# Moving 24 accumulating DRAM transfers of a fused two-block kernel out of its mixers on GpSimd's queue

## The reference, cut to what matters

```python
x = x + rms_norm(mix, ln_post_mix)          # norm 1, "post"
h = rms_norm(x, ln_pre_ffn)                 # norm 1, "pre"
f = (silu(h @ w_gate) * (h @ w_up)) @ w_down
x = x + rms_norm(f, ln_post_ffn)
```

## Time and profile before

| | us |
|---|---|
| median of 3 runs | 1268.55 |
| lowest and highest | 1266.91 and 1269.29 |
| the profiled execution, whole | 1270.42 |
| its span, first to last instruction | 1268.7 |
| PE busy in the span | 1254.4 |
| POOL busy in the span | 512.3 |

### The profile page before, as it was taken

One profiled execution on the slowest core, in us unless ns is written; L12 is line 12 of the kernel. 1 busy time (PEld: TensorE's weight loads), 2 busy tenths in 40 slices (PEclk: granted clock), 3 DMA queues, 4 the chain that ended last, 5 costly groups with the idle time before them and its releaser, 6 DMA issues.

```text
span 1268.7 us, 22131 instructions
## 1 busy us (share of the span) xinstructions
PE 1254.4 (99%) x7684; PEld 1142.8 (90%) x7684; DVE 949.8 (75%) x1732; ACT 729.0 (57%) x1437; POOL 512.3 (40%) x578
## 2 busy tenths in 40 slices
PE   8999999999999999999999999999999999999998
PEld 7999978989999988889999999889889999887887
DVE  6687765799988878884566778457987777789754
ACT  5666744545555556656667778435455555556452
POOL 5576781256655500126788866310121313000000
PEclk9999999999999999999999999999999999999999
DMA  7699732335444467522377953232323333565221
GB/s 232 223 202 235 170 92 100 99 132 202 165 132 165 142 239 217 141 76 76 67 159 139 166 105 89 95 103 90 100 83 93 103 98 99 197 242 166 68 99 67
DMA packets 145607, 173.45 MB, mean 137 GB/s; under 512 B 25420, under 2 KB 111643, under 8 KB 145522
## 3 DMA queue, kind: packets, MB, share of 16 engines
q1 hardware_dynamic: 129600, 145.15, 35.8%
q0 software_dynamic: 15920, 27.18, 12.1%
q10 hardware_dynamic: 2, 0.00, 0.0%
HBM read 170.22 MB, written 39.85 MB: 166 GB/s over the span
## 4 chain that ended last, share of the span: by engine, by line
PE 88%; DVE 6%; POOL 2%; ACT 1%; DMA 1%; issue 1%; ACTq 0%; DVEq 0%; POOLq 0%
PE ps L2844 13%; PE ps L2845 13%; PE ps L2846 13%; PE ps L2963 6%; PE ps L2970 6%; PE ps L2965 6%; PE ps L3096 3%; PE ps L3100 3%; PE ps L3098 3%; PE ps L3140 3%; PE ps L3142 3%; PE ps L3141 3%; PE ps L3058 2%; DVE w_lo L2393 2%; PE ps L3046 1%; PE ps L3047 1%
## 5 line engine op out<-in xcount | busy, mean ns | idle before, releaser
L2844 PE MATMUL ps<-h_hi,w_hi 128*128 128x256 f32 (+1 forms) x748 | 238.3, 319 | 0.0
L2845 PE MATMUL ps<-h_lo,w_hi 128*128 128x256 f32 (+1 forms) x748 | 237.4, 317 | 0.0
L2846 PE MATMUL ps<-h_hi,w_lo 128*128 128x256 f32 (+1 forms) x748 | 237.2, 317 | 0.0
L2963 PE MATMUL ps<-w_hi,h_hi 128*128 128x384 f32 (+2 forms) x512 | 162.6, 328 | 0.0
L2965 PE MATMUL ps<-w_hi,h_lo 128*128 128x384 f32 (+2 forms) x512 | 157.9, 319 | 0.0
L2846 PEld LDWEIGHTS ps<-h_hi,w_lo 128*128 128x128 f32 x748 | 142.6, 191 | 9.6
L2844 PEld LDWEIGHTS ps<-h_hi,w_hi 128*128 128x128 f32 x748 | 142.6, 191 | 9.1 <-DVE h_lo L2140 0.3
L2845 PEld LDWEIGHTS ps<-h_lo,w_hi 128*128 128x128 f32 x748 | 142.7, 191 | 8.5
L1281 POOL TENSOR_TENSOR w_lo<-w_raw,w_hi 128x384 fp32r<-128x384 f32 (+2 forms) x114 | 120.5, 1131 | 26.9 <-ACT w_hi L1524 26.7
L2970 PE MATMUL ps<-w_lo,h_hi 128*128 128x384 f32 (+2 forms) x512 | 101.5, 319 | 0.0
L3140 PE MATMUL ps<-w_hi,st_hi 128*128 128x512 f32 x252 | 98.6, 391 | 0.5 <-DVE st_lo L2404 0.2
(11 more groups left out here) (327 smaller groups left out, 3338.9 us busy)
## 6 DMA issues: line engine op xcount, KB each, us to landing
w_raw<-in_w_up_dram SPq DMA_DIRECT2D x25, 1024.0 KB, 5.3
w_raw<-in_w_in_dram SPq DMA_DIRECT2D x69, 256.0 KB, 4.1
w_raw<-in_w_gate_dram SPq DMA_DIRECT2D x11, 1024.0 KB, 5.3
down_sums<-in_w_down_dram SPq DMA_DIRECT2D x18, 512.0 KB, 5.9
down_sums<-in_w_down_dram SPq DMA_DIRECT2D x36, 256.0 KB, 6.0
down_sums<-in_w_down_dram POOLq DMA_DIRECT2D x12, 768.0 KB, 8.3
down_sums<-down_sums POOLq DMA_DIRECT2D x12, 768.0 KB, 8.7
w_raw<-in_w_out_dram SPq DMA_DIRECT2D x8, 1024.0 KB, 5.1
```

Source lines behind the costliest of these rows:

```text
L2844: pe.matmul(out_, s_hi, m_hi, start=first and n == 0, stop=False, skip_group_check=True)
L2845: pe.matmul(out_, s_hi, m_lo, start=False, stop=False, skip_group_check=True)
L2846: mm = pe.matmul(out_, s_lo, m_hi, start=False, stop=last and n == len(pairs) - 1, skip_group_check=True)
L2963: pe.matmul(bank, h_hi[:, kb0 + i, tok], hi[:, i, :], start=half == 0 and i == 0, stop=False, skip_group_check=True)
```

## The change

The transfers are no longer issued inside the mixers. Those of the first product go behind mixer 0: T1 and T3 of all groups ahead of the gain loads, T2 between the gain loads and norm 1, T4 behind norm 1. Those of the second go behind norm 3: T1 and T3 ahead of the first weight sums of the mixed gate and value products, T2 behind these, T4 behind the second. The loop over the other sums starts at 2 in place of 1.

```diff
-ADD_ORDER = ((0, "T1"), (0, "T3"), (0, "T2"), (1, "T1"), (0, "T4"), (1, "T3"),
-             (1, "T2"), (2, "T1"), (1, "T4"), (2, "T3"), (2, "T2"), (2, "T4"))
-ADD_AFTER = ((9, 12, 15, 18, 20, 23, 25, 27, 29, 32, 35, 38), (8, 11, 14, 17, 20, 23, 26, 29, 32, 35, 38, 41))
...
-                        normed_units += 1
-                        if normed_units in ADD_AFTER[mx.b]:
-                            sums_added(mx.b, *ADD_ORDER[ADD_AFTER[mx.b].index(normed_units)])
...
+            def sums_of_groups(d, *names):
+
+                for name in names:
+                    for g in range(GROUPS):
+                        sums_added(d, g, name)
...
             mixer(mixers[0])
+            sums_of_groups(0, "T1", "T3")
             pool.wait_ge(shared_filled, n1.n["shared"])
             gain(1, gain_post[:, :], "ln_post_mix")
             gain(2, gain_pre[:, :], "ln_pre_ffn")
+            sums_of_groups(0, "T2")
             norm(1, True)
+            sums_of_groups(0, "T4")
             block_sums(0, 0, first=True)
...
             norm(3, False)
+            sums_of_groups(1, "T1", "T3")
             gate_sums(0, first=True)
-            with pool.Fori(1, N_MIXED) as q:
+            sums_of_groups(1, "T2")
+            gate_sums(1)
+            sums_of_groups(1, "T4")
+            with pool.Fori(2, N_MIXED) as q:
                 gate_sums(q)
```

More of the change, by code:

```diff
@@ L1285, in mixer @@
                 own_n, own_d = mx.cnt.of[mx.steps[0]]["N"], 0
-                normed_units = 0
                 for s in mx.orders["pool"]:
```

## The result

The changed kernel takes 1289.49 us in the median of 4 runs (1287.62 to 1289.72); beside it the kernel before took 1268.92. The ratio is 1.0166 (95% interval 1.0152 to 1.0180): 20.6 us slower, where 15.2 were forecast.

A forecast was written before the change was run, and what follows sets the result against it. The prediction took PE to bound the kernel, busy 1254.4 of 1268.7 us. Its terms, -4.9 (mixers) + 20.1 (norm 1) + 0 (other places) = +15.2 us, took the median from 1268.55 to 1283.8 us, range 1270 to 1290.

The forecast's parts named there:

- The chain of the forecast: Norm 1: six transfers queued ahead make `gain_post` late, then DVE, then PE's first turn; the whole delay arrives, +20.1 us.
- the 3.4 us of cover: Norm 1: first `h_tok` ready at 215.3, PE's first turn at 218.76; the forecast said this 3.4 us isn't kept.
- signs of being wrong: `gain_post` landing within 10 us, PE's turn stall far shorter than DVE's wait, or new stalls in the second block's mixed products.
- The delay: Norm 1: `gain_post` lands at 229.3, DVE wants it at 209.22; 20.1 us late, between 11.3 and 24.3.
- The pitch of 4.5 us: POOL's DMA queue before norm 1: each 768 KB accumulating transfer takes 4.5 us, bounds 4.1 and 5.2; six take 27.0.
- the term of SP's loads: Ahead of `gain_post`: SP's loads of w_gate and w_up take 6.4 us of the same engines, all within the transfers' time.
- The order that rows showed: POOL's DMA queue: a load behind an accumulating transfer waits for it; a table load landed in 7.3 us against 3.1.
- the estimate in the prediction: Norm 1 by the skill's fit: six transfers in 10.8 us, `gain_post` at 213.1, delay 4 us, sum -0.9.
- The mixers: PE's `prob` stalls go, 2.9 and 0.3 us, and a half-clock stretch, 1.7 us: -4.9 us in all.
- The other new places: T2 before norm 1, T4 behind it, and the second block's transfers: PE waits for no load, 0 us, between 0 and 6.
- Rival 3: Data of T2 and T4 delay loads for either block's first sums, up to 6 us more: +25.4, 1294 us; chance 6%.

## Why the prediction was right, and where its sizes were off

**The mechanism.** The chain of the forecast stands: transfers ahead on POOL's queue, `gain_post` late, DVE's norm 1 late, the turn late, PE idle, and the whole delay kept. Of its signs, it said that DVE would wait about 20 us (19.69), `gain_post` take some 30 us (30.2), PE have one stall of about 17 us (13.9, which is the smaller delay of 17.4 less the 3.4 us of cover), and the second turn hide the slow stretch; all are in the trace. One of its signs of being wrong is there too: new stalls in the mixed products. Two experiments show the queue's part: another queue brings 30.2 to 8.0 us, and half the number ahead brings it to 15.5.

**The delay: 20.1 us forecast, 17.4 measured.** The pitch of 4.5 us was right: the three T1 landed 4.5 us apart in the mean. Too large was the term of SP's loads, added in full with 6.4 us. The three T3, which ran beside these loads, took 16.5 us, where three at the pitch of the T1 take 13.5, so the loads cost about 3 there. One reason is that by 222 us SP's queue had moved only 1.61 of the 2.10 MB; that the two queues also overlap is likely (over 189 to 222 us they had 89.8% and 17.2% of the engines, together more than 100%), but not shown, since a transfer alone can show a share above 100% as well. Against that, the first T1 took 0.5 us longer than its term.

The order that rows showed was right. The Trainium skill's fit for a transfer of this queue, 2.0 us and bytes at 436 GB/s (DMA: Bandwidth & Descriptors, "Anatomy of one DMA"), would by the estimate in the prediction have given a delay of 4 us. The trace doesn't agree for transfers that add within DRAM, 4.5 us each against the fit's 1.8 us of data, and the measurement decides. For plain copies within DRAM, 2.9 us each here, the fit is too short as well.

**The mixers: -4.9 us forecast, -4.3 and -1.3 in the traces, but only about 2 in the medians.** The mechanism was right for the first stall: moving one T4 takes it away. The size was read from one execution with a long stall and a slow stretch. Mixer 1 gave 1.3 us where I counted only PE's wait of 0.3, and moving its last T4 alone doesn't take that wait away.

**The other new places: 0 us forecast, +5.6 measured.** This is the step that failed: "PE waits for no load there, ACT's and DVE's splits and full buffers lie between. I put it at 0, between 0 and 6 us". A load that PE doesn't wait for had no 4 to 7 us to spare: the second 512 KB load went from 4.3 to 11.4 us and the 1 MB load from 6.6 to 13.5, and all of the cover was used up. Of the two kernels that move only transfers of the second product, one shows that the stalls don't come from the first block, the other that the T4s alone make the later one. Rival 3, with a chance of 6%, named this cost; it was wrong only in the delay of 24.3 us that it was added to. The same kind of loss stands behind norm 1, 6.4 us, but was covered by the gain's delay in the changed kernel; it showed when the gains no longer waited.

**What the trace doesn't hold.** In the traces the kernel is 17.2 us slower, in the medians 20.6. Some 2 us of the difference come from the changed kernel's side: its three other runs had clocks of 0.993 and 0.992 in place of 0.995 and took 1.8 to 2.1 us more than the profiled one. A slow stretch of 3.4 us at half clock costs 1.7 us; one stands at 977 us in the trace of the kernel with the gains first, behind the same stall at `w_lo`. That the changed kernel's slower runs have it there is likely, but no trace of them shows it. The rest of the 3.4 us is the kernel before, whose profiled run lies 1.5 us above its median. So the 15.2 came near the 17.2 by errors of opposite signs: the delay was put 2.7 us too high, the mixed products 5.6 too low, and the mixers' gain 0.7 too small. That is luck in part. So is the median, 1289.49, which lies only 0.5 us within the upper end of the range, 1290, and 5.7 us above the forecast 1283.8.

## What to carry to other kernels

Before moving transfers on a queue, list what stands behind them and when it is wanted: a small load behind six accumulating transfers of 768 KB came 26 us later, and one reordering or another queue avoids that, though the kernel stayed 9.0 and 9.9 us slower than before with them. Transfers off the critical path still take the engines from the loads beside them; ask of these loads how much later they may land, not whether somebody waits for them now. And where a term comes from a stall in a single profiled execution, look at whether its clock and time are those of the other runs.

## What the runs showed of the hardware

With the engines nearly to themselves, accumulating transfers of 768 KB from the weights into `down_sums` (T1) landed 4.6 and 4.3 us apart, those within `down_sums` (T4, behind norm 1 in the changed kernel) 3.8 us apart, and plain copies in place of the T1 3.0 and 2.9. Beside accumulating transfers, loads of 1 MB on SP's queue took 18.6 and 27.4 us in place of 5.2, while a load of 512 KB of gains with rows of 4 KB took only 8.0 there; what makes that difference was not tried. A stall of 2.9 us in front of PE's line 3058 was followed by 3.4 us at half clock in the first trace; stalls of 1.8 and 1.2 us at the same place, in the traces of the two kernels that change the second product alone, were not. In the second block a stall of 1.8 us was followed by such a stretch in one trace, and one of 2.5 us in the changed kernel's trace was not, so the length of the stall alone doesn't tell.
